# First four pooling tiles normalized inside the feed-forward's second pass; its results kept in SBUF and added by GpSimd; sums stored from SP

## The chip, the cores and the metric

One Trainium2 chip (trn2), one core of it. The metric is the device time of one execution in microseconds (us), lower is better. The engines are TensorE (PE, matmuls; PEld is its weight load), VectorE (DVE), ScalarE (ACT), GpSimd (POOL) and SyncE (SP, which here only issues DMAs). A DMA issued by SP is shown on the queue "hardware_dynamic", one issued by POOL on "software_dynamic".

## The reference

A two-layer backbone over 1024 tokens of width 1024, all in float32. Layer 0 is attention plus spatial gating and a dense SwiGLU feed-forward. Layer 1 begins with a pooling mixer and ends with a mixture of experts. The change sits between the two layers:

```python
x = x + mx[5] * _swiglu(_modulate(x, mx[3], mx[4]), w_gate, w_up, w_down)       # layer 0, dense feed-forward
...
x = x + mx[2] * _multiscale_pool(_modulate(x, mx[0], mx[1]), pool_w, pool_scale)  # layer 1, pooling mixer
x = x + mx[5] * _moe_swiglu(_modulate(x, mx[3], mx[4]), ...)                      # layer 1, experts
```

`_modulate(x, shift, scale)` is the row's RMS norm times (1 + scale) plus shift. `_multiscale_pool` takes, for four groups of 256 columns, centred means over 2, 4, 8 and 16 neighbouring tokens minus the token itself, multiplies each group by a 256x256 matrix and scales the columns.

## The kernel before, in words

The kernel is a sequence of phases. Each phase is a block with one instruction stream per engine; it ends with a barrier of all engines and a clearing of its semaphores by GpSimd (`phase_semaphores`), so that no engine begins a phase before every engine has finished the one before. Tokens are worked in tiles of 128 rows (`x[:, t, :]`, eight tiles).

**Feed-forward (`expert_mlp_phase` with the name "ffn").** Two passes of 512 tokens (four tiles); each pass runs 11 chunks of 256 hidden columns. In a chunk PE makes the gate and up products (`hidden`) and then the down products of the chunk before (`down`). ACT rounds weights and hidden values (`round_g`, `round_u`, `round_hidden`, `round_d`), DVE subtracts the rounded from the raw ones (`rest_g` and so on, L2413) and adds up the results in `y_t` (`add`, L2469). The chunks run in loops of pairs (`chunk_pairs`). At the end of a pass PE turns the sums, ACT and DVE write them to `y_out` (the tiles `dense_rows`, L2374 and L2584), and GpSimd adds each 128x1024 tile to the residual stream in DRAM (`x2`, shown as scratch_x) by an accumulating DMA (`add_result`, L2009). The DMAs of the last pass count up `dense_stored`. Rows of the tokens come in through `x_first`.

**Pooling (`pool_phase`).** SP loads the eight tiles of `x2` (L1232; the last four behind a wait on `dense_stored`), with shift and scale of layer 1 between the first and the second, and gate and column scales after them. For each tile: ACT squares and sums the row and takes the root (`first_norm`, L1310, L1312); DVE inverts it and modulates (`modulate`, L1379, L1388, L1389) into one of two buffers `h`; ACT rounds it to `h_hi` (`round_h`, L1316); DVE takes the rest `h_lo` (`split_h`, L1393). ACT also rounds the tables of the means (`band_hi` L1345, `edge_hi` L1346), and DVE their rest (`band_lo`, L1399). PE then multiplies by the tables (`difference`, L1267), turns the result (`turn`) and multiplies by the group matrices (`project`, L1291); a tile's `difference` needs `h` of the next tile too, so the first waits for two tiles. The order on ACT and DVE is written by hand: five tiles (`LEAD`) go ahead of PE, then one more in each step.

```python
            for t in range(LEAD):
                modulate(t)
                if t:
                    split_h(t - 1)
```

At the end of each tile DVE adds the gated result to x, ACT normalizes it for the experts (`norm`, L1343, `xn_rows`), and GpSimd stores both x and the normalized rows (L1244, L1245). GpSimd then waits until all sixteen stores have landed, and only then is the phase over.

**Routing (`routing_phase`)** begins with transposes of `xn_rows` on PE (L1536), and with SP's loads of the router's matrix (L1507) and of small tables.

## Time and profile before

| | |
|---|---|
| three runs, device time | 3943.25 to 3946.82 us, median 3946.48 |
| the profiled execution: its own time | 3940.43 us |
| its span, first to last instruction | 3938.4 us, mean granted TensorE clock 0.959 |
| busy share of the span | PE 92%, PEld 84%, DVE 58%, ACT 42%, POOL 8% |
| last matmul of the feed-forward to first of pooling | 1361.7 to 1396.2 us |
| pooling, first to last instruction | 1376.4 to 1470.0 us |
| first instruction of routing | 1475.6 us |

The profile is of one execution. Its times are microseconds from the start of the span. A row of the timeline gives start, duration, engine, line, operation and tiles, and in brackets how long the engine sat idle just before and on whom it waited. Windows give the busy time of each engine in a stretch, then the clock that was granted to TensorE (1.00 is the full 2.4 GHz, 0.50 is 1.2 GHz). Landing is the time from the issue of a DMA until its data are there.

### The profile page before, as it was taken

To read this page: it belongs to the slowest core of one execution; us is meant where nothing else is said; L and a number is where in the kernel's file an instruction comes from. 1 tells how busy PE (TensorE), PEld (TensorE's weight loads), DVE (VectorE), ACT (ScalarE), POOL (GpSimd) and SP (SyncE) were. 2 spreads that over 40 slices of the span, in tenths; PEclk is the share of its full clock that TensorE was granted. 3 is DMA by queue.
4 is the path that set the end of the run, shared out by engine and by line. 5 is a ranking of instruction groups with operands and counts; after the bars stand their busy time and mean duration, and the time that the engine had idled before them with its cause. 6 is when DMAs were issued, how large, how long until landed. Compare 5 with 4: busy or idle time off the path is not lost. (4 is left out here: it accounts for less than half of the span.)

```text
span 3938.4 us, 61110 instructions
## 1 busy us (share of the span) xinstructions
PE 3622.0 (92%) x22550; PEld 3318.8 (84%) x22551; DVE 2275.8 (58%) x2997; ACT 1662.4 (42%) x1943; POOL 296.5 (8%) x247
## 2 busy tenths in 40 slices
PE   7989897999999865999999999989999899999995
PEld 4986576888888653989999999988899898998995
DVE  3557634444444364866655555558565697665665
ACT  4225524222322153754443343347443465444444
POOL 0006401000000001010010010000100100000001
PEclk8999998999999987999999999999999999999997
DMA  6513325332322134974454354459543665545553
GB/s 220 214 56 113 121 75 202 98 98 96 107 96 96 46 147 147 357 236 173 160 174 140 137 162 138 143 165 367 184 156 131 182 245 183 181 160 150 199 174 137
DMA packets 408821, 627.11 MB, mean 159 GB/s; under 512 B 18227, under 2 KB 332211, under 8 KB 408616
## 3 DMA queue, kind: packets, MB, share of 16 engines
q1 hardware_dynamic: 384136, 534.68, 39.1%
q0 software_dynamic: 24192, 88.98, 7.7%
q8 instruction: 88, 1.44, 0.2%
q14 instruction: 117, 0.96, 0.1%
q10 hardware_dynamic: 288, 1.05, 0.1%
HBM read 579.46 MB, written 46.15 MB: 159 GB/s over the span
## 5 line engine op out<-in xcount | busy, mean ns | idle before, releaser
L2413 DVE TENSOR_TENSOR moe_gu_lo<-moe_raw_gu_lo,moe_gu_hi 128x2048 fp32r<-128x2048 f32 x254 | 580.7, 2286 | 160.9 <-ACT moe_gu_hi L2262 160.5
L2262 ACT ACTIVATE moe_gu_hi<-moe_raw_gu_lo 128x2048 fp32r<-128x2048 f32 x254 | 485.9, 1914 | 276.6 <-DMA moe_raw_gu_lo<-in_moe_w_gate 224.2
L2102 PE MATMUL moe_g<-moe_x,moe_gu_hi 128*128 128x336 f32 (+4 forms) x1344 | 416.9, 310 | 29.0 <-issue 20.3
L2469 DVE SCALAR_TENSOR_TENSOR moe_y_t<-moe_y,moe_cols,moe_y_t 128x288 f32<-128x288 f32 (+4 forms) x728 | 372.6, 536 | 105.7 <-PE moe_y L2104 105.1
L2104 PE MATMUL moe_g<-moe_x,moe_gu_lo 128*128 128x336 f32 (+4 forms) x1344 | 415.3, 309 | 0.0
L2103 PE MATMUL moe_g<-moe_x,moe_gu_hi 128*128 128x336 f32 (+4 forms) x1344 | 415.2, 309 | 0.0
L2102 PE MATMUL moe_y<-moe_h,moe_d_hi 128*128 128x336 f32 (+4 forms) x1344 | 412.5, 307 | 2.8 <-DVE moe_y_t L2465 2.8
L2102 PE MATMUL moe_u<-moe_x,moe_gu_hi 128*128 128x336 f32 (+4 forms) x1344 | 410.2, 305 | 0.0
L2104 PE MATMUL moe_u<-moe_x,moe_gu_lo 128*128 128x336 f32 (+4 forms) x1344 | 410.0, 305 | 0.0
L2104 PE MATMUL moe_y<-moe_h,moe_d_lo 128*128 128x336 f32 (+4 forms) x1344 | 409.9, 305 | 0.0
L2103 PE MATMUL moe_u<-moe_x,moe_gu_hi 128*128 128x336 f32 (+4 forms) x1344 | 409.6, 305 | 0.0
L2103 PE MATMUL moe_y<-moe_h,moe_d_hi 128*128 128x336 f32 (+4 forms) x1344 | 409.5, 305 | 0.0
L2449 DVE TENSOR_TENSOR moe_h_full<-moe_h_full,moe_u 128x336 f32<-128x336 f32 (+4 forms) x168 | 80.4, 479 | 483.8 <-PE moe_u L2104 483.8
L2413 DVE TENSOR_TENSOR moe_d_lo<-moe_raw_d_lo,moe_d_hi 128x2048 fp32r<-128x2048 f32 x126 | 287.7, 2284 | 10.8 <-ACT moe_d_hi L2262 10.8
L2102 PEld LDWEIGHTS moe_g<-moe_x,moe_gu_hi 128*128 128x128 f32 x1344 | 259.1, 193 | 31.1 <-issue 31.1
L2294 ACT ACTIVATE moe_h<-moe_h_full 128x336 fp32r<-128x336 f32 (+5 forms) x196 | 87.0, 444 | 456.9 <-DVE moe_h_full L2449 456.9
L2103 PEld LDWEIGHTS moe_g<-moe_x,moe_gu_hi 128*128 128x128 f32 x1344 | 258.4, 192 | 0.0
L2104 PEld LDWEIGHTS moe_g<-moe_x,moe_gu_lo 128*128 128x128 f32 x1344 | 258.4, 192 | 0.0
L2102 PEld LDWEIGHTS moe_y<-moe_h,moe_d_hi 128*128 128x128 f32 x1344 | 253.7, 189 | 3.5 <-DVE moe_y_t L2465 3.5
L2102 PEld LDWEIGHTS moe_u<-moe_x,moe_gu_hi 128*128 128x128 f32 x1344 | 254.0, 189 | 0.0
L2104 PEld LDWEIGHTS moe_u<-moe_x,moe_gu_lo 128*128 128x128 f32 x1344 | 253.3, 188 | 0.0
L2103 PEld LDWEIGHTS moe_u<-moe_x,moe_gu_hi 128*128 128x128 f32 x1344 | 253.2, 188 | 0.0
(388 smaller groups left out, 8169.3 us busy)
## 6 DMA issues: line engine op xcount, KB each, us to landing
moe_raw_gu_lo<-in_moe_w_gate SPq DMA_DIRECT2D x127, 1024.0 KB, 4.9
moe_raw_gu_lo<-in_moe_w_up SPq DMA_DIRECT2D x127, 1024.0 KB, 7.1
...
```

The costliest lines, as they stand in the source:

```text
L2102: pe.matmul(bank[:, 0:width], wh, moving[:, 0, 0:width], start=start, stop=False)
L2103: pe.matmul(bank[:, 0:width], wh, moving[:, 1, 0:width], start=False, stop=False)
L2104: return pe.matmul(bank[:, 0:width], wl, moving[:, 0, 0:width], start=False, stop=stop)
L2262: act.activation(hi[par][:, :, :], raw[par][:, :, :], ACT.Copy).then_inc(rounded, 1)
L2294: act.activation(h[par][:, f, 0, 0:width], h_full[:, f, 0:width], ACT.Copy).then_inc(h_rounded, 1)
L2413: dve.tensor_tensor(lo[par][:, :, :], raw[par][:, :, :], hi[par][:, :, :].bitcast(F), ALU.subtract).then_inc(split, 1)
L2449: dve.tensor_tensor(h_full[:, f, 0:width], h_full[:, f, 0:width], up, ALU.mult)\
L2469: dve.scalar_tensor_tensor(y_t[:, db, 0:cols], y_ps[db % 4][:, 0:cols], gate, y_t[:, db, 0:cols], ALU.mult, ALU.add).then_inc(y_added, 1)
```

## The change

1. **In the feed-forward's second pass** (`load_pooled`, `pooled_squares`, `pooled_roots`, `modulate_pooled`) the four tiles of tokens that the first pass has finished are normalized and modulated for pooling. GpSimd reloads them from `x2` into `x_first`, and shift and scale of layer 1 into two tiles of `y_out` that stand empty; ACT squares them between chunks 3 and 4 and between chunks 5 and 6 and takes all roots in one instruction; DVE modulates two tiles after chunk 7 and two after chunk 9. `chunk_pairs` of that pass is split on ACT (three loops for one) and on DVE (two for one).
2. **The last pass's results are not added in DRAM.** The four accumulating DMAs are gone; the tiles stay in `dense_rows`, and in pooling GpSimd adds them to the four loaded tiles (`added`). `x` of pooling (`keep["pool_x"]`) is no longer a tile of the phase alone.
3. **In pooling** ACT and DVE begin with the rounding and the rests of four tiles that are ready (`READY` = 4); only tile 4 is normalized ahead of the loop. SP loads tiles 4 to 7 first. The two squares' buffers are tiles of their own.
4. **SP stores** x and the normalized rows instead of GpSimd, and pooling no longer waits until they have landed: SP waits for them (`pool_stored`) in routing, behind its loads.

```diff
         @block.sync
         def _(sp):
-            for t in range(TX):
-                if t == TX - TILES_PASS:
-                    for stored in keep["dense_stored"]:
-                        sp.wait_ge(stored, 16)
+            for t in (*range(READY, TX), *range(READY)):
                 sp.dma_start(x[:, t, :], dram["x2"][t * P:(t + 1) * P, :]).then_inc(x_ld[t], 16)
-                if t == 0:
+                if t == READY:
                     for i, to in enumerate((shift, scale)):
                         sp.dma_start(to[:, :], dram["pool_mod"][i, :].partition_broadcast(P)).then_inc(mod_ld, 16)
...
+            for t in range(TX):
+                sp.wait_ge(normed, t + 1)
+                sp.dma_start(dram["x3"][t * P:(t + 1) * P, :], x[:, t, :]).then_inc(x_st, 16)
+                sp.dma_start(dram["xn"][t * P:(t + 1) * P, :], x_norm[:, t, :]).then_inc(x_st, 16)
 
         @block.gpsimd
         def _(pool):
 
-            for t in range(TX):
-                pool.wait_ge(normed, t + 1)
-                pool.dma_start(dram["x3"][t * P:(t + 1) * P, :], x[:, t, :]).then_inc(x_st, 16)
-                pool.dma_start(dram["xn"][t * P:(t + 1) * P, :], x_norm[:, t, :]).then_inc(x_st, 16)
-            pool.wait_ge(x_st, 32 * TX)
+            for t in range(READY, TX):
+                pool.wait_ge(x_ld[t], 16)
+                pool.tensor_tensor(x[:, t, :], x[:, t, :], keep["dense_rows"][:, t - READY, :], ALU.add).then_inc(added, 1)
...
+            round_h(0)
             act.activation(band_hi[:, :, :, :], band[:, :, :, :], ACT.Copy).then_inc(tables_ok, 1)
+            round_h(1)
             act.activation(edge_hi[:, :, :, :], edge[:, :, :, :], ACT.Copy).then_inc(tables_ok, 1)
+            for t in range(2, READY):
+                round_h(t)
             act.wait_ge(eps_ok, 1)
-            for t in range(LEAD):
-                first_norm(t)
-                if t:
-                    round_h(t - 1)
+            first_norm(READY)
             copy(0)
...
+            split_h(0)
+            dve.wait_ge(tables_ok, 1)
+            dve.tensor_tensor(band_lo[:, :, 0:3:2, :], band[:, :, 0:3:2, :], band_hi[:, :, 0:3:2, :].bitcast(F), ALU.subtract)\
+               .then_inc(band_ok, 1)
+            for t in range(1, READY):
+                split_h(t)
             dve.wait_ge(mod_ld, 32)
             link(dve.tensor_scalar(scale[:, :], scale[:, :], 1.0, None, ALU.add))
...
+            modulate(READY)
...
             sp.dma_start(tile_starts[:, :], dram["tile_starts"].partition_broadcast(P)).then_inc(ld, 16)
+            sp.wait_ge(keep["pool_stored"], 32 * TX)
...
+            def load_pooled():
+
+                pool.memset(pooled["early_eps"][:, :], EPS).then_inc(pool_ready, 1)
+                for t in range(TILES_PASS):
+                    pool.wait_ge(y_stored[t], 16)
+                    if t >= 2:
+                        pool.dma_start(y_out[:, t, :], pool_mod[t - 2, :].partition_broadcast(P)).then_inc(pool_mod_ld, 16)
+                pool.wait_ge(x_turned, passes * KD + X0)
+                for t in range(TILES_PASS):
+                    pool.dma_start(pool_h_in[:, t, :], x2[t * P:(t + 1) * P, :]).then_inc(pool_x_ld, 16)
...
+                def pooled_squares(tiles):
+
+                    act.wait_ge(pool_x_ld, TILES_PASS * 16)
+                    act.wait_ge(y_stored[1], 16)
+                    for t in tiles:
+                        if t:
+                            act.wait_ge(pool_squared, t)
+                        act.activation(pool_square, pool_h_in[:, t, :], ACT.Square, accum_out=pooled["early_sums"][:, t:t + 1])\
+                           .then_inc(pool_squared, 1)
...
+                if has_next(p):
+                    chunk_pairs(act, p, 0, C - 2, step)
+                else:
+                    chunk_pairs(act, p, 0, C - 8, step)
+                    pooled_squares(range(2))
+                    chunk_pairs(act, p, C - 7, C - 6, step)
+                    pooled_squares(range(2, TILES_PASS))
+                    pooled_roots()
+                    chunk_pairs(act, p, C - 5, C - 2, step)
...
+                def modulate_pooled(t):
+
+                    row = pool_h_in[:, t, :]
+                    dve.scalar_tensor_tensor(row, row, pooled["early_rstd"][:, t:t + 1], pool_scale, ALU.mult, ALU.mult)\
+                       .then_inc(pool_scaled, 1)
+                    dve.wait_ge(pool_scaled, t + 1)
+                    dve.tensor_tensor(row, row, pool_shift, ALU.add).then_inc(pool_h, 1)
...
+                    chunk_pairs(dve, p, 2, C - 4, step)
+                    dve.wait_ge(pool_mod_ld, 32)
+                    dve.tensor_scalar(pool_scale, pool_scale, 1.0, None, ALU.add).then_inc(pool_ready, 1)
+                    dve.wait_ge(pool_rooted, 1)
+                    dve.reciprocal(pooled["early_rstd"][:, :], pooled["early_root"][:, :]).then_inc(pool_ready, 1)
+                    dve.wait_ge(pool_ready, 3)
+                    modulate_pooled(0)
+                    modulate_pooled(1)
+                    chunk_pairs(dve, p, C - 3, C - 2, step)
+                    modulate_pooled(2)
+                    modulate_pooled(3)
```

How DVE's instructions stand at the start of pooling, before:

```order
L1395 MEMSET pool_eps 128x1
L1397 TENSOR_SCALAR pool_scale<-pool_scale 128x1024
L1399 TENSOR_TENSOR pool_band_lo<-pool_band,pool_band_hi 128x4x2x128
L1379 RECIPROCAL pool_rstd<-pool_root 128x1
L1388 SCALAR_TENSOR_TENSOR pool_scaled<-pool_x,pool_rstd,pool_scale 128x1024
L1389 TENSOR_TENSOR x_first<-pool_scaled,pool_shift 128x1024
L1379 RECIPROCAL pool_rstd<-pool_root 128x1
L1388 SCALAR_TENSOR_TENSOR pool_scaled<-pool_x,pool_rstd,pool_scale 128x1024
L1389 TENSOR_TENSOR x_first<-pool_scaled,pool_shift 128x1024
L1393 TENSOR_TENSOR pool_h_lo<-x_first,pool_h_hi 128x1024
```

and in the changed kernel, up to the first wait for a product of PE:

```order
L1401 MEMSET pool_eps 128x1
L1399 TENSOR_TENSOR pool_h_lo<-x_first,pool_h_hi 128x1024
L1404 TENSOR_TENSOR pool_band_lo<-pool_band,pool_band_hi 128x4x2x128
L1399 TENSOR_TENSOR pool_h_lo<-x_first,pool_h_hi 128x1024 x3
L1409 TENSOR_SCALAR pool_scale<-pool_scale 128x1024
L1386 RECIPROCAL pool_rstd<-pool_root 128x1
L1394 SCALAR_TENSOR_TENSOR pool_scaled<-pool_x,pool_rstd,pool_scale 128x1024
L1395 TENSOR_TENSOR x_first<-pool_scaled,pool_shift 128x1024
L1386 RECIPROCAL pool_rstd<-pool_root 128x1
L1394 SCALAR_TENSOR_TENSOR pool_scaled<-pool_x,pool_rstd,pool_scale 128x1024
L1395 TENSOR_TENSOR x_first<-pool_scaled,pool_shift 128x1024
L1399 TENSOR_TENSOR pool_h_lo<-x_first,pool_h_hi 128x1024
```

Behind the memset, twelve instructions and a wait for shift and scale stood ahead of the second `pool_h_lo`, which PE needs; now the first two `pool_h_lo` and `pool_band_lo` are DVE's first three operations.

How GpSimd's instructions stand around the end of the feed-forward and in pooling, before (the pair L1244, L1245 comes eight times in all):

```order
L2009 DMA scratch_x<-dense_rows 128x1024 x8
L1786 UNCONDITIONAL_BRANCH
L101 ISA
L1239 UNCONDITIONAL_BRANCH
L1244 DMA scratch_x<-pool_x 128x1024
L1245 DMA scratch_xn<-xn_rows 128x1024
```

and in the changed kernel:

```order
L2022 DMA scratch_x<-dense_rows 128x1024 x4
L2026 MEMSET early_eps 128x1
L2030 DMA dense_rows<-scratch_pool_mod 128x1024 x2
L2033 DMA x_first<-scratch_x 128x1024 x4
L1795 UNCONDITIONAL_BRANCH
L101 ISA
L1243 UNCONDITIONAL_BRANCH
L1248 TENSOR_TENSOR pool_x<-pool_x,dense_rows 128x1024 x4
```

GpSimd leaves the feed-forward with loads that belong to the start of the second pass as its last DMAs, and in pooling it computes where it stored.

## Rows read from the trace of the kernel before

**Rows 1.** Windows: busy us (count) per engine, TensorE clock, DMA share, GB/s
```profile
1100.00:1300.00 200.00, 200.00 (x884) 165.62 (x883) 89.44 (x90) 48.54 (x43) 0.00 (x0) 1.00 0.29 94
...
1361.00:1367.00 6.00, 0.66 (x7) 0.42 (x4) 1.21 (x2) 0.60 (x1) 2.55 (x3) 1.00 0.99 158
1367.00:1396.00 29.00, 0.00 (x0) 0.00 (x0) 11.80 (x14) 12.29 (x18) 0.00 (x0) 0.50 0.79 257
1396.00:1401.00 5.00, 4.63 (x20) 4.34 (x20) 4.84 (x7) 3.11 (x7) 0.00 (x0) 0.50 0.00 0
1401.00:1466.00 65.00, 55.58 (x356) 50.46 (x356) 45.60 (x55) 40.74 (x73) 6.36 (x12) 1.00 0.25 98
```

**Rows 2.** Timeline at the feed-forward's end, and landing of its four accumulating DMAs
```profile
1361.70 0.69 DVE L2584 TENSOR_SCALAR dense_rows<-ffn_y 128x512 f32<-128x512 f32 x1 [0.18 <-PE ffn_y L2162]
...
DMA to landing us min/median/max: 5.4/9.3/12.3
```

**Rows 3.** Timeline at the boundary from attention to its output phase
```profile
469.69 0.42 DVE L786 COPY att<-att_out_ps 128x256 f32<-128x256 f32 x1 [1.42 <-PE att_out_ps L740]
470.84 0.37 SPq L935 DMA_DIRECT2D mix_w_s<-in_gm_w_s  x1
```

**Rows 4.** Timeline of ACT, DVE and PE at the start of pooling
```profile
1376.45 1.48 ACT L1345 ACTIVATE pool_band_hi<-pool_band 128x1536 fp32r<-128x1536 f32 x1 [14.60 <-PEq L102]
...
1379.87 1.06 ACT L1310 ACTIVATE x_first<-pool_x 128x1024 f32<-128x1024 f32 x1 [0.99 <-DMA pool_x<-scratch_x]
...
1381.04 1.28 ACT L1312 ACT_TABLE_LOAD   x1
...
1385.27 1.06 ACT L1310 ACTIVATE x_first<-pool_x 128x1024 f32<-128x1024 f32 x1 [2.65 <-DMA pool_x<-scratch_x]
...
1391.16 1.22 DVE L1393 TENSOR_TENSOR pool_h_lo<-x_first,pool_h_hi 128x1024 fp32r<-128x1024 f32 x1
...
1396.25 0.58 PE L1267 MATMUL pool_diff_ps<-pool_h_hi,pool_band_hi 128*128 128x256 f32 x1 [34.59 <-DVE pool_h_lo L1393]
```

**Rows 5.** Timeline of POOL and DVE in the output phase
```profile
3907.39 10.25 POOL L1733 TENSOR_TENSOR moe_y<-moe_y,moe_rows 128x1024 f32<-128x1024 f32 x4 [257.34 <-POOLq L102]
...
3912.01 3.43 DVE L1763 SCALAR_TENSOR_TENSOR out_early<-out_early,out_rstd,out_gain 128x1024 f32<-128x1024 f32 x1
...
3915.54 3.18 DVE L1763 SCALAR_TENSOR_TENSOR out_early<-out_early,out_rstd,out_gain 128x1024 f32<-128x1024 f32 x1
...
3918.83 1.28 DVE L1763 SCALAR_TENSOR_TENSOR out_early<-out_early,out_rstd,out_gain 128x1024 f32<-128x1024 f32 x1
```

**Rows 6.** Timeline of PE in pooling: a stall that has nothing ahead of it
```profile
1421.76 0.36 PE L1267 MATMUL pool_diff_ps<-pool_h_hi,pool_band_hi 128*128 128x256 f32 x1 [1.58 <-ACT pool_diff L1328]
```

**Rows 7.** Timeline from pooling to routing, and landing of the stores of xn_rows
```profile
1467.52 1.15 ACT L1343 ACTIVATE xn_rows<-pool_x,pool_rstd 128x1024 f32<-128x1024 f32 x1 [0.30 <-DVE pool_rstd L1379]
...
1469.49 0.53 POOL L1245 DMA_DIRECT2D scratch_xn<-xn_rows  x1
...
1475.59 0.38 SPq L1507 DMA_DIRECT2D route_router<-in_router_w  x1
...
1478.07 1.78 PE L1526 MATMUL route_logit_t_ps<-route_h,route_router 128*8 128x512 f32 x2 [0.49 <-DMA route_router<-in_router_w]
...
DMA to landing us min/median/max: 3.8/3.8/3.8
```

**Rows 8.** Timeline of ACT, DVE and PE late in the second pass
```profile
1286.66 0.60 ACT L2287 ACTIVATE ffn_h_full<-ffn_g 128x512 f32<-128x512 f32 x1 [8.67 <-PE ffn_g L2104]
...
1292.10 0.69 DVE L2449 TENSOR_TENSOR ffn_h_full<-ffn_h_full,ffn_u 128x512 f32<-128x512 f32 x1 [7.75 <-PE ffn_u L2104]
1292.70 2.29 DVE L2413 TENSOR_TENSOR ffn_gu_lo<-ffn_raw_gu_lo,ffn_gu_hi 128x2048 fp32r<-128x2048 f32 x1
...
1313.66 0.39 PE L2102 MATMUL ffn_g<-ffn_x,ffn_gu_hi 128*128 128x512 f32 x1
```

**Rows 9.** Waits of the whole span: ACT's time in which it waited for nothing shown
```profile
ACT L2262 <- issue: 86.6, 9, 15.1
```

87 lines of the change are left out of this document (52 added, 35 removed).

## The prediction

> **What bounds the kernel now.** I read the windows first, because the busy share of the whole span says nothing about a stage. In the feed-forward PE is busy 200.00 of 200.00 us, with DVE at 89.44 and ACT at 48.54 [rows 1]: there PE is the bound and the other two have room. From 1367 to 1396 PE is at zero; from 1401 to 1466, in pooling, it is busy 55.58 of 65 us, DVE 45.60 and ACT 40.74 [rows 1]. So the places to win are the hole before pooling and the joints, and inside pooling PE paces again.
>
> The timeline names what ends the hole: PE sits 34.59 us until DVE's `pool_h_lo` [rows 4], and it splits it. DVE's last work in the feed-forward ends at 1361.70 + 0.69 = 1362.39, and nothing of pooling starts before ACT at 1376.45, after 14.60 us of idling [rows 4]; the accumulating DMAs, issued around 1360 to 1364, take up to 12.3 us to land [rows 2], and DMAs are busy 0.99 of the time there [rows 1]. That is 14.1 us of joint. At the joint from attention to its output phase, where GpSimd has no DMA in flight, last work and first work are 470.11 and 470.84, 0.73 us apart [rows 3]. I read the 13.3 us between the two as GpSimd not leaving its phase before its own DMAs are done. Then 1376.45 to 1396.25, 19.8 us, pass inside pooling until PE starts: loads, and norms and modulations on ACT and DVE [rows 4]. At the end ACT is done at 1467.52 + 1.15 = 1468.67 and routing begins at 1475.59: 6.9 us, of which most is the last store, issued at 1469.49 and 3.8 us in landing [rows 7].
>
> **The change, part by part.** The sum is made against the profiled execution, 3940.4 us; the median of the runs, 3946.5, stands 6.1 us above it, and I carry the difference over to the median.
>
> *Work moved into the second pass: 0.* ACT gets four squares (1.06 us each in pooling [rows 4], with the reading of the sum a little more), two at a place, with the root behind the second pair, some 4 us, and table changes in the loop after it; DVE gets two modulations at a place, 4 x about 1.25 plus a scale and an inversion, some 6 us. ACT idles 8.67 us and DVE 7.75 us while PE makes a chunk's first products, and weights split by 1292.70 + 2.29 = 1294.99 are first used at 1313.66, 18.7 us later [rows 8]. Nothing else waits for these rows until pooling. The cover is that slack; without it the whole work would show: on ACT 4 x 1.25 for squares, 0.3 for the root and five table loads of 1.28 [rows 4], 11.7 us; on DVE 4 x 2.5 + 0.9 = 10.9 us. GpSimd's six loads (3 MB) come right after the first pass's additions, when the next thing anybody needs of them is four chunks off; on GpSimd nothing is queued behind them.
>
> *Joint to pooling: -13.3.* No DMA of GpSimd is in flight at the end now, so 14.1 us should become 0.73. Bounds: -13.3, and -11.8 if the joint costs what the one after pooling costs beyond the landing (1469.49 + 3.8 = 1473.3 to 1475.59, 2.3 us [rows 7]).
>
> *Start of pooling until PE's first product: -12.5.* What must come first now is two roundings and two tables on ACT, and three subtractions on DVE. ACT: h(0) at 1.0 us, `band_hi` to 2.4, h(1) to 3.4, `edge_hi` to 4.4 (1.48 us for the wide table and 1.06 for a tile [rows 4], each overlapping the next by some 0.1). DVE: h_lo(0) to 2.2, `band_lo` 2.4 to 3.6, h_lo(1) to 4.8. So PE could start at 4.8 instead of 19.8: -15.0. But the first of tiles 4 to 7 arrives where tile 0 does now, 3.4 us into the phase (1379.87 against 1376.45 [rows 4]), and then GpSimd adds, 10.25 / 4 = 2.56 us each [rows 5]. In the output phase DVE's 128x1024 operation with two tiles from SBUF lasts 1.28 us alone but 3.43 and 3.18 us while GpSimd adds [rows 5]. The first addition starts just when h_lo(1) is due, and holds it to about 6.1; PE starts at 7.3. Bounds: 4.8 without the meeting, 7.3 with it; I take 7.3, since the output phase shows the same pair of operations.
>
> The Trainium skill ("SBUF — State Buffer", SBUF: two separate sides) says that the port pair which VectorE and GpSimd share is an exclusive lock, held for the whole instruction, also against a VectorE operation with two SBUF inputs: the loser fully blocks. It speaks against this change; the trace agrees (3.43 for 1.28 us). Taken to its end, it gives the rival of full cost below.
>
> *Rest of pooling: +1.0.* PE's order is untouched, its products are the same, and its stall of 1.58 us behind ACT's copy [rows 6] comes from tile 6's modulation standing behind the first result on DVE, which stays so. The granted clock was 0.50 when PE restarted at 1396.25, with PE idle since about 1361.7, and 1.00 from 1401 [rows 1]; before, it was still 1.00 up to 1367. PE will be idle some 9 us now, past that point, so I assume the same slow 5 us. New is that additions 2 to 4, from about 8.8 us on (second tile now: 1385.27 - 1376.45 [rows 4]), meet tile 4's modulation, and ACT must round it before it copies tile 1's differences. That copy is due at about 16 us. A modulation that takes two blocks of 2.0 us ends between 14 and 17. Bounds -1.6 (the stall gone) and +2.6 (one whole addition more); I take +1.0.
>
> *Joint to routing: -5.2.* SP issues the last two stores in 0.4 us each (0.38 for its router load [rows 7]) and goes; 0.9 + 0.73 = 1.7 us after ACT instead of 6.9. *Router's matrix: +1.5.* PE already waits 0.49 us for it, 2.5 us after its issue [rows 7]. Now 1 MB of stores is ahead of it, landing 3.8 us after the last issue, 4.7 us after ACT's end, where the router used to need 1.7 + 2.4 = 4.1. So it comes between 0 and 3.0 us later than it could (0.6 to 3.0 if it queues); I take 1.5. Small tables are needed much later. The Trainium skill ("DMA: Bandwidth & Descriptors", Queues, rings and completion order) says that an engine consumes a ring's descriptors in order, and by it the sum would have the upper half of that range; no row here shows it.
>
> Sum: -13.3 - 12.5 + 1.0 - 5.2 + 1.5 = **-28.5 us**. That is 3911.9 for an execution like the profiled one, and 3946.5 - 28.5 = **3918.0** for the median.
>
> **The rivals.** *Forecast, 58%: 3918.0.*
>
> *The additions miss DVE, 13%.* If tile 4 lands late or DVE wins the race for the start, PE begins at 4.8 and nothing is delayed later: -13.3 - 15.0 - 5.2 + 1.5 = -32.0, 3914.5. For it: a delay of half a microsecond in the load decides. Against: the blocks in the output phase were not avoided by DVE once [rows 5].
>
> *Each addition costs the path in full, 16%.* Four additions by 2.0 us (3.43 and 3.18 less 1.28 [rows 5]) make 8.1 in place of the 3.5 that I count: -23.9, 3922.6. DVE would be the bound of the first 20 us. Against: between the additions DVE waits for roots anyway. This is what the lock rule of the Trainium skill's SBUF page makes of it if all four meet DVE.
>
> *The joint does not shrink, 6%.* If the 14.1 us are not the accumulating DMAs but code loading or another fixed cost of leaving this phase, then -28.5 + 13.3 = -15.2, 3931.3. Against: the other joint with 0.73 us [rows 3].
>
> *The change does not hide what it moves, 4%.* If the 12 us on ACT and 11 us on DVE stand on PE's path, -28.5 + 23 = -5.5, 3941.0, which is no change. Against: 200.00 us busy of 200.00 with DVE at 45% [rows 1].
>
> *Slower, 3%.* ACT enters two loops more in the second pass and DVE one, three new pieces of code. ACT's wait for nothing shown reaches 15.1 us elsewhere [rows 9]. Each such stall is free up to 18.7 us [rows 8] and stops PE beyond. The change is lost when each of the three takes 18.7 + 28.5/3 = 28.2 us, and slower by 0.2% from 31 us; at 35 us each it would be 3946.5 - 28.5 + 3 x 16.3 = 3966.9. It would need twice the longest stall on record.
>
> **How the numbers follow.** About 0.2% of this kernel, 7.9 us, is what a measurement can tell from no change. The range: all good ends are -13.3 - 15.0 - 1.6 - 5.2 + 0 = -35.1 (3911.4), all bad ends of the forecast are -11.8 - 12.5 + 2.6 - 5.2 + 3.0 = -23.9 (3922.6), which is also the time of the rival of full cost. The runs of the kernel before spread over 3.6 us, and a TensorE clock that stays low some 5 us longer would cost about 2.5; I set 3908 to 3928, which leaves out the joint, the unhidden work and the slower case, 13%, and a little. Faster by over 0.2%: 58 + 13 + 16 + 6 = 93%; within: 4%; slower: 3%.
>
> **What would show it.** Right: pooling's first instruction 0.7 to 2.3 us after the feed-forward's last; PE's first difference about 7 us later with DVE's second `pool_h_lo` at 3 us or more; `TENSOR_TENSOR pool_x` on POOL about 2.6 us; the same PE pace after that; routing 1.7 us after ACT, PE waiting for the router 1 to 3 us; PE in the second pass 100% busy at clock 1.00. Wrong: a joint of over 5 us, a gap of PE in the second pass, PE's first difference before 5.5 or after 9 us, or a pooling phase whose steps from one gated result to the next are longer than before.

## The result, and the profile after

| | before | changed |
|---|---|---|
| median device time | 3946.32 us (4 runs, 3943.25 to 3946.82) | 3906.67 us (4 runs, 3902.22 to 3907.56) |
| profiled execution, its span | 3940.43 us, 3938.4 | 3906.23 us, 3904.5 |
| ratio of the times | | 0.9896, 95% interval 0.9881 to 0.9910 |

The change is faster by 39.65 us where 28.5 were forecast. The time lies 1.3 us below the range. So the direction was right and the size was not, and as the stages show the sum was wrong in both directions: one term gave back more than I had allowed for, and a stage that the change does not touch got shorter. How much shorter the kernel is differs between series of runs as well: in a later one the same two kernels took 3940.14 and 3908.84 us, 31.3 us apart (ratio 0.9919, 0.9904 to 0.9933; the run a_again below).

**Where the time went, by stage.** I cut both profiled executions at the same eight events. Each cut can be read in the rows; those of after follow below.

| stretch, us | before | after | difference | forecast |
|---|---|---|---|---|
| start to DVE's last result of the feed-forward | 1362.39 | 1363.24 | +0.85 | 0 |
| from there to pooling's first instruction on ACT | 14.06 | 0.91 | -13.15 | -13.3 |
| to PE's first product | 19.80 | 7.04 | -12.76 | -12.5 |
| to the end of ACT's last `xn_rows` | 72.42 | 78.42 | +6.00 | +1.0 |
| to SP's load of the router's matrix | 6.92 | 1.77 | -5.15 | -5.2 |
| routing, up to GpSimd's first copy for the experts | 56.64 | 58.39 | +1.75 | +1.5 |
| experts' phase, up to GpSimd's additions of the output | 2375.16 | 2364.11 | -11.05 | 0 |
| output, to the end of the span | 31.01 | 30.62 | -0.39 | 0 |
| sum | 3938.4 | 3904.5 | -33.9 | -28.5 |

The medians lie further apart than these two executions, since the profiled one of before was 5.9 us under its median and the one of after only 0.4. The +0.85 of the first line is scatter: in the other executions of kernels whose feed-forward is that of before, the same point lies between 1361.8 and 1365.1 us.

The windows of the changed kernel, with the columns of [rows 1], show that the moved work is hidden: in 200 us that hold the first three groups of moved work, PE is still busy all the time at clock 1.00, while ACT rose from 48.54 to 61.44 and DVE from 89.44 to 95.06.

```profile
1090.00:1290.00 200.00, 200.00 (x884) 165.62 (x883) 95.06 (x96) 61.44 (x58) 0.00 (x0) 1.00 0.29 96
```

The timeline at the joint answers to [rows 2, 4]: DVE's last result of the feed-forward, ACT's first rounding, and PE's first product.

```profile
1362.55 0.69 DVE L2658 TENSOR_SCALAR dense_rows<-ffn_y 128x512 f32<-128x512 f32 x1 [0.18 <-PE ffn_y L2188]
...
1364.15 1.06 ACT L1321 ACTIVATE pool_h_hi<-x_first 128x1024 fp32r<-128x1024 f32 x1 [1.44 <-PEq L102]
...
1371.19 0.58 PE L1270 MATMUL pool_diff_ps<-pool_h_hi,pool_band_hi 128*128 128x256 f32 x1 [8.68 <-DVE pool_h_lo L1399]
```

The next rows are the place where 5 us more than forecast went: the timeline of DVE, GpSimd, ACT and PE in the first 21 us of pooling.

```profile
1367.45 2.61 POOL L1248 TENSOR_TENSOR pool_x<-pool_x,dense_rows 128x1024 f32<-128x1024 f32 x1 [352.17 <-DMA pool_x<-scratch_x]
1372.79 8.96 POOL L1248 TENSOR_TENSOR pool_x<-pool_x,dense_rows 128x1024 f32<-128x1024 f32 x3 [2.74 <-DMA pool_x<-scratch_x]
...
1367.76 5.66 DVE L1399 TENSOR_TENSOR pool_h_lo<-x_first,pool_h_hi 128x1024 fp32r<-128x1024 f32 x3
1373.33 2.87 DVE L1409 TENSOR_SCALAR pool_scale<-pool_scale 128x1024 f32<-128x1024 f32 x1
...
1376.43 3.13 DVE L1394 SCALAR_TENSOR_TENSOR pool_scaled<-pool_x,pool_rstd,pool_scale 128x1024 f32<-128x1024 f32 x1
1379.60 3.25 DVE L1395 TENSOR_TENSOR x_first<-pool_scaled,pool_shift 128x1024 f32<-128x1024 f32 x1
...
1382.95 1.28 DVE L1394 SCALAR_TENSOR_TENSOR pool_scaled<-pool_x,pool_rstd,pool_scale 128x1024 f32<-128x1024 f32 x1
...
1382.88 1.06 ACT L1321 ACTIVATE pool_h_hi<-x_first 128x1024 fp32r<-128x1024 f32 x1 [5.56 <-DVE x_first L1395]
1383.84 1.06 ACT L1333 ACTIVATE pool_diff<-pool_diff_ps 128x512 f32<-128x512 f32 x2
...
1385.05 0.55 PE L1270 MATMUL pool_diff_ps<-pool_h_hi,pool_band_hi 128*128 128x256 f32 x1 [4.97 <-ACT pool_diff L1333]
```

The last three additions come back to back, 8.96 us, and three DVE operations in a row, the scale and tile 4's modulation, take 2.87, 3.13 and 3.25 us; the same operation as the second takes 1.28 as soon as GpSimd has stopped, in the row at 1382.95. Tile 4 is late by that. ACT has to round tile 4 before it copies tile 1's differences, so it idles 5.56 us and then copies, and PE, which had caught up, waits 4.97 us for that copy. The windows after it show a second price: TensorE's granted clock falls back to 0.50 in the stretch where PE restarts, as it had at the first start. In the timeline PE's first 15 products from 1385.05 on take 3.28 us, where later ones start every 0.12 us; that is about 1.5 us lost (an estimate from these rows).

```profile
1382.00:1384.00 2.00, 0.00 (x0) 0.00 (x0) 1.96 (x3) 1.12 (x2) 0.00 (x0) 1.00 0.06 23
1384.00:1386.00 2.00, 0.95 (x4) 0.98 (x5) 1.97 (x3) 2.00 (x5) 0.00 (x0) 0.70 0.00 0
1386.00:1388.00 2.00, 2.00 (x12) 2.00 (x11) 0.63 (x1) 1.97 (x4) 0.00 (x0) 0.50 0.00 0
1388.00:1390.00 2.00, 2.00 (x18) 2.00 (x18) 0.00 (x0) 1.07 (x3) 0.00 (x0) 0.94 0.00 0
```

The joint to routing, beside [rows 7]: routing begins 1.77 us after ACT, and PE waits 0.94 us for the router's matrix, which was 0.49.

```profile
1448.46 1.15 ACT L1348 ACTIVATE xn_rows<-pool_x,pool_rstd 128x1024 f32<-128x1024 f32 x1 [0.30 <-DVE pool_rstd L1386]
...
1451.38 0.38 SPq L1515 DMA_DIRECT2D route_router<-in_router_w  x1
...
1454.31 1.88 PE L1535 MATMUL route_logit_t_ps<-route_h,route_router 128*8 128x512 f32 x2 [0.94 <-DMA route_router<-in_router_w]
```

The matrix thus costs 0.45 of routing's 1.75 us. The rest goes with TensorE's clock. Windows of before, from 4.4 us into routing, and of the changed kernel, from 3.6 to 10.6 us into it:

```profile
1480.00:1500.00 20.00, 20.00 (x79) 6.66 (x78) 0.68 (x1) 10.10 (x13) 0.00 (x0) 1.00 0.04 8
```

```profile
1455.00:1462.00 7.00, 7.00 (x20) 2.15 (x18) 0.00 (x0) 1.91 (x3) 0.00 (x0) 0.65 0.12 22
```

In windows of 2 us the changed kernel still has 0.50 from 1456 to 1458 and 0.52 from 1458 to 1460, up to 8.6 us into the phase. DVE's first copy of the router's products comes 17.39 us into routing and came 15.10 us into it before; about half a microsecond of that is made up by the end of the phase.

**The experts' phase** is bounded by two rows of GpSimd, of before (the second is the first of [rows 5]):

```profile
1532.23 0.19 POOL L2705 COPY token_now<-token_of 128x4 int32<-128x4 int32 x1 [62.21 <-POOLq L1994]
```

and of the changed kernel:

```profile
1509.77 0.19 POOL L2783 COPY token_now<-token_of 128x4 int32<-128x4 int32 x1 [128.01 <-POOLq L2008]
...
3873.88 11.24 POOL L1742 TENSOR_TENSOR moe_y<-moe_y,moe_rows 128x1024 f32<-128x1024 f32 x4 [253.85 <-POOLq L102]
```

Nothing in the code of this phase differs. What differs is in the waits. Of before, ACT's idle time without a releaser at L2262 is 86.6 us with a longest of 15.1 [rows 9], and PE has this row:

```profile
PE moe_u L2192 <- DVE moe_h_full L2483: 14.3, 4, 8.5
```

In the changed kernel the two read:

```profile
ACT L2288 <- issue: 52.3, 9, 8.9
...
PE moe_u L2218 <- DVE moe_h_full L2536: 10.9, 5, 3.4
```

The timeline has one such pair. Before, at the end of a pass of the experts, ACT finishes at 2621.48 and begins the next chunk at 2631.60, 10.12 us in which it waited for nothing that the profile knows; PE stands still for 8.53 us up to 2638.88, until DVE has worked on what ACT prepares after that.

```profile
2620.79 0.69 ACT L2374 ACTIVATE moe_y<-moe_y,weight_now 128x512 f32<-128x512 f32 x1 [0.66 <-PE moe_y L2162]
...
2631.60 1.28 ACT L2262 ACT_TABLE_LOAD   x1 [10.12 <-issue]
...
2638.88 0.69 PE L2192 MATMUL moe_u<-ident,moe_h_full 128*128 128x128 f32 x2 [8.53 <-DVE moe_h_full L2483]
```

After, at the same place of the same pass, ACT waited 4.80 us:

```profile
2597.59 0.69 ACT L2427 ACTIVATE moe_y<-moe_y,weight_now 128x512 f32<-128x512 f32 x1 [0.67 <-PE moe_y L2188]
...
2603.08 1.28 ACT L2288 ACT_TABLE_LOAD   x1 [4.80 <-issue]
```

The queue q14, which the profile names "instruction", carried less, 117 packets before and 101 after.

That gave Theory 1: the change put 71 more instructions on ACT and 49 more on DVE ahead of the experts' code (a count of the two programs), and where this code lies in memory sets how long an engine waits for it. The rival was that the phase differs by chance from execution to execution.

### The profile page after: what moved, and what is told of

It is laid out like the page before. It is cut to its first block and busy times, and to the rows that moved or that the text cites. A ratio compares the mean times of both kernels' runs of the same rounds, so it can differ in the third digit from the quotient of the medians.

```text
span 3904.5 us, 61076 instructions
## 1 busy us (share of the span) xinstructions
PE 3620.8 (93%) x22550; PEld 3316.3 (85%) x22551; DVE 2284.8 (59%) x2995; ACT 1668.4 (43%) x1945; POOL 300.9 (8%) x238
## 5 line engine op out<-in xcount | busy, mean ns | idle before, releaser
L2128 PEld LDWEIGHTS moe_y<-moe_h,moe_d_hi 128*128 128x128 f32 x1344 | 253.1, 188 | 2.0 <-DVE moe_y_t L2518 2.0
L2130 PEld LDWEIGHTS moe_y<-moe_h,moe_d_lo 128*128 128x128 f32 x1344 | 253.7, 189 | 0.0
L2129 PEld LDWEIGHTS moe_y<-moe_h,moe_d_hi 128*128 128x128 f32 x1344 | 253.2, 188 | 0.0
```

The costliest lines, as they stand in the source:

```text
L2128: pe.matmul(bank[:, 0:width], wh, moving[:, 0, 0:width], start=start, stop=False)
L2129: pe.matmul(bank[:, 0:width], wh, moving[:, 1, 0:width], start=False, stop=False)
L2130: return pe.matmul(bank[:, 0:width], wl, moving[:, 0, 0:width], start=False, stop=stop)
```

## The experiments

The expectations speak of "the experts' phase" with its ends taken between the first and last instruction of a phase, which gives 0.1 us more than the table above. Most runs were executed several times and have an interval against the kernel before on the same chip; the three runs on the joint and a_double are one execution each.

### Padding: code moved, nothing else

An unused semaphore is increased on ACT at the end of routing and on DVE at its start; "b_" is made from the kernel before, "a_" from the changed one. The change also moved GpSimd's and SP's code, by 12 instructions fewer and 14 more; the padding leaves that out.

```diff
+            for _ in range(71):
+                act.sem_inc(padded[0], 1)
...
+            for _ in range(49):
+                dve.sem_inc(padded[1], 1)
```

> The kernel before with nothing of the change, but with 71 semaphore increments added on ScalarE behind its last work in routing and 49 on VectorE ahead of its first work there, both while the engine waits, so that the experts' code stands as many instructions further on as in the changed kernel. Theory 1 (the expert phase's 11 us come from where its code stands): from routing's end to the output phase 2364 us instead of 2375, ScalarE's idle time with nothing shown to wait for some 52 us instead of 87, and the whole 7 to 12 us faster than before. Theory 2 (the 11 us are a difference between executions, or come from the rows' stores going through SP): 2375 us there, time within 3 us of before.

> The changed kernel with 185 increments more on ScalarE and 207 more on VectorE at the same two places of routing. Theory 1: the expert phase changes again, by some us in either direction (toward 2375 us if the place repeats itself every 256 instructions, since 71 + 185 and 49 + 207 are 256), so 3900 to 3920 us. Theory 2: 2364 us in the expert phase and 3906 to 3908 us in all.

> The kernel before with 71 increments of an unused semaphore on ScalarE alone, at the end of routing. With the increments on both ScalarE (71) and VectorE (49) the phase of the experts took 2367.4 us instead of 2375.2. Theory: ScalarE's code place sets it, since ScalarE's idle time at L2262 without a releaser fell most (86.6 to 48.0 us in its group): then this run gives the whole gain, experts' phase 2366 to 2369 us and 3930 to 3934 us in all. Rival: VectorE's place sets it: then this run is like the kernel before, 2374 to 2376 us and 3940 to 3944. Second rival: each has a share.

> The kernel before with 49 increments on VectorE alone, at the start of routing. Theory (ScalarE's place): nothing, experts' phase 2374 to 2376 us, 3940 to 3944 us in all. Rival (VectorE's place): the whole gain, 2366 to 2369 us, 3930 to 3934.

| run | ACT, DVE moved by | median | before, same chip | ratio (95%) | experts' phase | ACT's idle time without releaser at the experts' weights: sum, longest | q14 packets |
|---|---|---|---|---|---|---|---|
| before | 0, 0 | 3946.32 | | | 2375.2 | 86.6, 15.1 | 117 |
| b_pad | 71, 49 | 3932.51 | 3942.54 | 0.9975 (0.9965 to 0.9985) | 2367.3 | 48.0, 8.8 | 101 |
| b_pad_act | 71, 0 | 3934.88 | 3941.91 | 0.9980 (0.9971 to 0.9989) | 2364.8 | 53.7, 8.7 | 107 |
| b_pad_dve | 0, 49 | 3938.79 | 3941.91 | 0.9993 (0.9984 to 1.0002) | 2373.6 | 74.4, 13.5 | 110 |
| changed | 71, 49 | 3906.67 | 3946.32 | 0.9896 (0.9881 to 0.9910) | 2364.1 | 52.3, 8.9 | 101 |
| a_pad | 256, 256 | 3917.80 | 3942.54 | 0.9936 (0.9922 to 0.9949) | 2377.7 | 76.7, 14.9 | 121 |

The cuts of b_pad, from the timeline of GpSimd, and its row of the waits:

```profile
1535.23 0.19 POOL L2710 COPY token_now<-token_of 128x4 int32<-128x4 int32 x1 [61.78 <-POOLq L1999]
...
3902.52 11.24 POOL L1738 TENSOR_TENSOR moe_y<-moe_y,moe_rows 128x1024 f32<-128x1024 f32 x4 [259.59 <-POOLq L102]
...
ACT L2267 <- issue: 48.0, 8, 8.8
```

Increments that do nothing make the kernel before faster by 10.0 us, with an interval clear of 1. In the changed kernel others go the other way: a_pad's ratio, 0.9936, is clear of the changed kernel's 0.9896, but it is not clear of that kernel's 0.9919 in a later series (0.9904 to 0.9933), so its size is open; the medians are 9 to 11 us apart. So the place of the code moves the time. ACT's part is the larger one by the medians, 7.0 us; DVE's 3.1 us has an interval that includes no effect, so whether it has a share is not decided; the two together agree with b_pad. Moved by 256, ACT's longest wait is back where it was at 0 (14.9 for 15.1 us), which fits places that repeat every 256 instructions, but one point does not prove a period.

How much of the 11.05 us is it? The length of the phase in one execution does not say. The profiled execution of b_pad_act was the fastest of its eleven, 7.8 us under their median, and that of b_sp_stores, a run below that moves nothing on ACT and DVE, has 2370.5 us with ACT's waits as long as before (88.2, longest 14.8). A window over the phase splits it into the time in which PE is busy with its 15648 products and the time in which it is not:

| experts' phase, us | length | PE busy | PE idle |
|---|---|---|---|
| before, place 0 | 2375.2 | 2253.3 | 121.9 |
| b_sp_stores, place 0 | 2370.5 | 2244.0 | 126.5 |
| b_pad, place 71 | 2367.3 | 2253.0 | 114.3 |
| b_pad_act, ACT alone at 71 | 2364.8 | 2244.3 | 120.5 |
| b_pad_dve, DVE alone at 49 | 2373.6 | 2250.4 | 123.2 |
| changed, place 71 | 2364.1 | 2249.5 | 114.6 |
| a_again, place 71 | 2368.8 | 2253.4 | 115.4 |
| a_both_p57, place 128 | 2376.7 | 2252.7 | 124.0 |
| a_pad, place 256 | 2377.7 | 2252.4 | 125.3 |

PE's busy time differs by up to 9 us between executions, whatever the place; it is scatter. The idle time goes with the place: 121.9 and 126.5 us at 0, 114.3 to 119.5 in the nine executions with both engines at their places in the changed kernel or within four instructions of them, 124.0 at 128 and 125.3 at 256. So of the 11.05 us between the two profiled executions, 7.3 are less idle time, as in b_pad (7.6), and 3.7 are scatter of the executions. That ACT alone has the larger part rests on the medians; in b_pad_act's one profile PE's idle time is only 1.4 us below that of before.

### What holds a phase open: GpSimd's own DMAs

Three kernels look at the joint behind the feed-forward. Made from the changed one, they copy or add the last four tiles to unused rows in DRAM as well, and nobody but GpSimd, behind its additions, waits for them.

```diff
+                for t in range(TILES_PASS):
+                    pool.wait_ge(y_left, (passes - 1) * TILES_PASS + t + 1 + O0)
+                    pool.wait_ge(y_right, (passes - 1) * TILES_PASS + t + 1 + O0)
+                    pool.dma_start(pooled["x3_spare"][t], y_out[:, t, :]).then_inc(pooled["copy_stored"], 16)
...
+            pool.wait_ge(keep["copy_stored"], 16 * TILES_PASS)
```

In a_joint_sp the same three lines stand on SP; in a_joint_acc the DMA has `accum_op=ALU.add`, onto rows filled in the first chunks of the second pass.

> The changed kernel with four 128x1024 tiles of the feed-forward's last pass also copied to unused rows in DRAM by GpSimd's own DMAs, as late as before, and waited for only in pooling by GpSimd behind its additions. Nobody waits for these data at the joint. Theory: GpSimd itself doesn't leave a phase while its own DMAs are in flight; then the joint from the feed-forward's last instruction to pooling's first is 12 to 14 us again instead of 0.9, and the whole 3917 to 3921 us. Rival: the joint was long because someone waited for the data of the accumulating DMAs; then it stays 0.9 us, and the whole is within 2 us of 3906.

> The same four copies, issued by SP on the hardware queue at the same place. Theory: only GpSimd's own DMAs hold it; the joint stays 0.9 us, at most 1 to 2 us more for the four issues, the whole 3905 to 3909 us. Rival: any DMA in flight at the end of a phase holds it, 12 to 14 us, the whole 3917 to 3921 us.

> The changed kernel with the four tiles of the last pass added to unused rows in DRAM by GpSimd with an accumulating DMA, as before the change but with nobody waiting for them except GpSimd behind its additions. The plain copies on the same queue landed in 3.6 us and the joint was 6.1 us from VectorE's end; from SP's queue 1.4 us. Theory: GpSimd leaves the phase when its own DMAs have landed, and accumulating ones take 9 us; then VectorE's end to pooling's first instruction is 12 to 15 us. Rival: the accumulation itself doesn't matter, 6 us as with the copies, and the rest of the 14 us before was the wait of SP for the data.

DVE's last row of the feed-forward, ACT's first of pooling, and the copies with their median time to landing, of a_joint_pool:

```profile
1362.26 0.69 DVE L2663 TENSOR_SCALAR dense_rows<-ffn_y 128x512 f32<-128x512 f32 x1 [0.18 <-PE ffn_y L2193]
...
1369.04 1.06 ACT L1322 ACTIVATE pool_h_hi<-x_first 128x1024 fp32r<-128x1024 f32 x1 [6.62 <-PEq L102]
...
scratch_x<-dense_rows POOLq DMA_DIRECT2D x4, 512.0 KB, 3.6
```

of a_joint_sp, with PE's first product and GpSimd's first addition:

```profile
1361.36 0.69 DVE L2664 TENSOR_SCALAR dense_rows<-ffn_y 128x512 f32<-128x512 f32 x1 [0.18 <-PE ffn_y L2194]
...
1363.48 1.06 ACT L1322 ACTIVATE pool_h_hi<-x_first 128x1024 fp32r<-128x1024 f32 x1 [1.96 <-PEq L102]
...
1368.35 0.58 PE L1271 MATMUL pool_diff_ps<-pool_h_hi,pool_band_hi 128*128 128x256 f32 x1 [7.04 <-DVE pool_h_lo L1400]
...
1368.81 3.43 POOL L1248 TENSOR_TENSOR pool_x<-pool_x,dense_rows 128x1024 f32<-128x1024 f32 x1 [354.53 <-DMA pool_x<-scratch_x]
...
scratch_x<-dense_rows SPq DMA_DIRECT2D x4, 512.0 KB, 3.1
```

and of a_joint_acc:

```profile
1363.86 0.69 DVE L2666 TENSOR_SCALAR dense_rows<-ffn_y 128x512 f32<-128x512 f32 x1 [0.18 <-PE ffn_y L2196]
...
1377.83 1.06 ACT L1322 ACTIVATE pool_h_hi<-x_first 128x1024 fp32r<-128x1024 f32 x1 [13.80 <-PEq L102]
...
scratch_x<-dense_rows POOLq DMA_DIRECT2D x4, 512.0 KB, 8.8
```

| | DVE's end to ACT's start | the profiled execution |
|---|---|---|
| changed | 0.91 | 3906.2 |
| copies from SP | 1.43 | 3902.0 |
| copies from GpSimd | 6.09 | 3913.3 |
| additions in DRAM from GpSimd | 13.28 | 3924.1 |
| before | 14.06 | 3940.4 |

My expectation for the copies from GpSimd, 12 to 14 us, missed: I had taken the landing time of the accumulating DMAs (median 9.3 us [rows 2]) for that of any DMA. The two others came in at the joint. These are single executions, but the joint scatters little: 0.91 us in the changed kernel and in five others whose GpSimd has nothing in flight there, 12.0 to 14.1 in the five kernels that keep the additions of before. The joint follows the landing of GpSimd's own DMAs, 3.6 us each or 8.8, though nobody waits for the data. The same copies from SP hold almost nothing: the last was issued at 1362.1, none landed in under 2.7 us, and pooling began at 1363.48, while it was under way. The 14 us were thus two facts at once: GpSimd doesn't leave the phase while its DMAs are under way, and adding in DRAM takes more than twice as long as copying. Which of GpSimd's instructions does the waiting no row shows.

a_joint_sp also answers another question. There the first addition began at 1368.81, after the second `pool_h_lo` (1.22 us, ended at 1368.30), and PE's first product came 4.87 us into pooling instead of 7.04, with the additions still on GpSimd. So it is the meeting of these two that costs PE's start 2.2 us.

### The stall in pooling: two repairs

a_dve_add gives the four additions to DVE, at the places where it would otherwise wait; a_act_order leaves them on GpSimd and lets ACT round tile 4 only after it has copied tile 1's differences.

```diff
-            for t in range(READY, TX):
-                pool.wait_ge(x_ld[t], 16)
-                pool.tensor_tensor(x[:, t, :], x[:, t, :], keep["dense_rows"][:, t - READY, :], ALU.add).then_inc(added, 1)
...
+            def add_rows(t):
+                dve.wait_ge(x_ld[t], 16)
+                dve.tensor_tensor(x[:, t, :], x[:, t, :], keep["dense_rows"][:, t - READY, :], ALU.add).then_inc(added, 1)
```

```diff
-                if t + LEAD <= TX:
+                if t and t + LEAD <= TX:
                     round_h(t + LEAD - 1)
...
                 copy_turned(t)
+                if t == 0:
+                    round_h(LEAD - 1)
```

> The changed kernel with the four additions of the kept rows on VectorE instead of GpSimd: tile 4's behind the second rest, tile 5's ahead of tile 4's modulation, the other two behind tile 4's rest. If VectorE is held by GpSimd's additions: all its 128x1024 operations at the start of pooling take 1.1 to 1.3 us, TensorE's first difference comes 4.8 us into the phase instead of 7.0, its stall of 5.0 us behind ScalarE's copy goes, and pooling is 6 to 8 us shorter; 3899 to 3901 us. If the additions are hidden whatever engine does them: no change or up to 3 us more, for 4 x 1.15 us more on VectorE.

> The changed kernel with one instruction moved on ScalarE: tile 4's rounding behind the copies of the first step instead of ahead of them. If TensorE's 5.0 us stall comes from the copy standing behind a rounding that waits for VectorE: the stall goes, the granted clock does not fall again at 1385, and pooling is 4 to 6 us shorter with VectorE's operations still stretched to 3.1 us; 3901 to 3903 us. If VectorE is the bound of the start anyway: under 1 us.

> The changed kernel with the additions on VectorE and with tile 4's rounding behind the copies of the first step on ScalarE, the two edits measured singly. The additions on VectorE gave 2.2 us before PE's first product and 4.4 us behind it, the order on ScalarE 6.4 us behind it. Theory: both shorten the same stall of PE near 20 us into pooling (GpSimd's and VectorE's crossing makes tile 4 late, ScalarE's order passes that on to PE), so behind PE's first product no more than 7 us go, and with the 2.2 us before it some 9 us in all in pooling; 3896 to 3902 us if the experts' phase stays 2364 to 2368 us. Rival: two separate stalls, the gains add, 13 us, 3892 to 3895.

| us | pooling's first instruction to PE | PE to ACT's last `xn_rows` | both | experts' phase | median | ratio (95%) |
|---|---|---|---|---|---|---|
| before | 19.80 | 72.42 | 92.2 | 2375.2 | 3946.32 | |
| changed | 7.04 | 78.42 | 85.5 | 2364.1 | 3906.67 | 0.9896 (0.9881 to 0.9910) |
| a_dve_add | 4.9 | 74.0 | 78.9 | 2368.0 | 3902.76 | 0.9895 (0.9880 to 0.9910) |
| a_act_order | 7.0 | 72.0 | 79.0 | 2366.7 | 3903.75 | 0.9898 (0.9882 to 0.9913) |
| a_both | 4.9 | 74.2 | 79.1 | 2370.2 | 3902.36 | 0.9900 (0.9885 to 0.9915) |

The timeline of a_dve_add, PE's first product, the second addition between the scale and tile 4's modulation on DVE, and ACT's end:

```profile
1369.60 0.58 PE L1268 MATMUL pool_diff_ps<-pool_h_hi,pool_band_hi 128*128 128x256 f32 x1 [6.52 <-DVE pool_h_lo L1397]
...
1372.87 0.69 DVE L1413 TENSOR_SCALAR pool_scale<-pool_scale 128x1024 f32<-128x1024 f32 x1
1373.69 1.23 DVE L1401 TENSOR_TENSOR pool_x<-pool_x,dense_rows 128x1024 f32<-128x1024 f32 x1
...
1375.03 1.29 DVE L1392 SCALAR_TENSOR_TENSOR pool_scaled<-pool_x,pool_rstd,pool_scale 128x1024 f32<-128x1024 f32 x1
...
1442.48 1.15 ACT L1346 ACTIVATE xn_rows<-pool_x,pool_rstd 128x1024 f32<-128x1024 f32 x1 [0.30 <-DVE pool_rstd L1384]
```

Without GpSimd beside it, the scale is back at 0.69 us for 2.87 and the modulation at 1.29 for 3.13, and an addition costs DVE 1.23 us, less than the 2 us that one on GpSimd costs it in waiting. In a_act_order the DVE operations are as long as in the changed kernel:

```profile
1375.66 3.08 DVE L1396 SCALAR_TENSOR_TENSOR pool_scaled<-pool_x,pool_rstd,pool_scale 128x1024 f32<-128x1024 f32 x1
1378.77 3.31 DVE L1397 TENSOR_TENSOR x_first<-pool_scaled,pool_shift 128x1024 f32<-128x1024 f32 x1
```

but the chain from them to PE is cut, the granted clock stays at 1.00 from 1376 on, and pooling is as short. Each repair takes 6.4 to 6.6 us off the whole of pooling, and both together no more (79.1): they remove one stall, not two. That is even less than the 9 us that I expected of both, since the 2.2 us before PE's first product are lost again behind it. The windows show where. In the changed kernel the clock is back at 1.00 in the window that begins 4.8 us after PE's first product; in a_dve_add it is still 0.50 in the one that begins 6.4 us after it, and 0.86 in the next:

```profile
1376.00:1378.00 2.00, 1.90 (x16) 1.93 (x17) 1.93 (x3) 1.29 (x3) 2.00 (x1) 1.00 1.03 412
```

```profile
1376.00:1378.00 2.00, 2.00 (x11) 2.00 (x11) 1.93 (x4) 0.79 (x4) 0.00 (x0) 0.50 1.03 414
```

PE starts earlier and then works some 5 us longer at half the clock, about 2 us lost by an estimate from these rows; a_both has the same 0.50 there. Why the clock comes back later in these two is not shown.

The whole, expected at 3899 to 3901, 3901 to 3903 and 3896 to 3902 us, came out at 3902.76, 3903.75 and 3902.36, each a little above. Their ratios are that of the changed kernel in its first series (0.9896) and better than the one in a later series (0.9919), so the 6.4 us are shown in the stage and not in the whole. The experts' phase was 3 to 6 us longer than 2364.1 in these executions, but the changed kernel itself had 2368.8 in another, so nothing follows from that.

### The stores moved alone

b_sp_stores is the kernel before with part 4 of the change only: SP stores, and waits for the landing in routing.

> The kernel before with only part 4 of the change: SP stores x and the normalized rows, pooling doesn't wait for their landing. Theory: the joint from pooling to routing shrinks by 5 us as in the changed kernel (from 5.6 to 1.0 us behind the last instruction), routing gives 1 to 2 us back while PE waits for the router's matrix behind the stores, 3 to 4 us faster in all apart from the experts' phase. Rival: SP's loads queue behind the stores and routing gives it all back, 0.

3937.47 us against 3940.48 on the same chip, ratio 0.9996 (0.9987 to 1.0005), which doesn't tell the 3 to 4 us expected from nothing. Its stages do, with the cuts of the first table: from ACT's last `xn_rows` to SP's load 1.74 us for 6.92, and routing 58.33 for 56.64, PE waiting 0.99 us for the router's matrix and the clock at 0.50 up to 7.6 us into the phase. That is -5.2 and +1.7, the same as in the changed kernel, so both terms belong to this part. It changes two things at once, though, the engine that stores and the wait for the landing, which the kernel before had in its code; which of them held the phase is not separated.

### Is the moved work hidden with room

a_double squares each of the four tiles twice and modulates it twice in the second pass.

> The changed kernel with each of the four tiles squared twice on ScalarE and modulated twice on VectorE inside the feed-forward's second pass: about 4 us more on ScalarE and 16 us more on VectorE. Theory: the second pass is bound by TensorE and both have more slack than that; the feed-forward stays 749.8 us, within 0.5. Rival (the work moved there is hidden only just): the feed-forward grows by 2 to 15 us.

The window of the feed-forward's two passes, of a_double:

```profile
600.00:1363.00 763.00, 738.36 (x3301) 611.62 (x3300) 368.32 (x376) 232.85 (x230) 16.36 (x24) 0.98 0.33 108
```

and of the changed kernel:

```profile
600.00:1363.00 763.00, 738.29 (x3301) 611.49 (x3300) 358.36 (x368) 228.32 (x222) 16.31 (x24) 0.98 0.33 108
```

DVE did 9.96 us more (I had written 16; four modulations of 2.5 us are 10) and ACT 4.53, and the last result of the feed-forward came at 1363.31 instead of 1363.24. The cover has room for twice the work. (The whole took 3912.35 us, and the experts' phase of that execution 2370.2.)

### Looking for a better place

The version with both repairs was run with 57, 20 and 226 more increments on ACT, and the changed kernel once more on the chip of the last two.

> The same kernel with 57 increments of an unused semaphore on ScalarE at the end of routing. So far ScalarE's code moved by 71 instructions gave 8 to 11 us in the experts' phase and by 256 nothing; this run stands at 128. Theory (ScalarE's code place, returning every 256 instructions): another value of the experts' phase, between 2360 and 2378 us, which differs from that of the same kernel without increments by more than 2 us. Rival (a place is either good or bad by chance of the execution): within 2 us of it.

> The version with both edits and 20 increments on ScalarE, so that its code stands at 91 against the kernel before; 71 gave 2364 to 2370 us in the experts' phase, 128 gave 2377, 0 and 256 2375 to 2378. Theory (the cost of a place changes smoothly with it): 2364 to 2374 us and 3898 to 3908 in all. Rival (a place near 71 isn't special; single places are good): anything from 2360 to 2378.

> The same version with 226 increments, which is the place 297, or 41 if places return every 256 instructions. Theory: a value between those of 0 and 71, 2366 to 2374 us. Rival: no return every 256, any value from 2360 to 2378; at 256 it was 2377.7.

> The changed kernel itself, on the chip of the next two. Theory (the pooling stage of the version with both edits is 6.4 us shorter and its experts' phase 6 us longer): the two kernels are within 2 us of each other, 3902 to 3907 us where the kernel before takes 3940 to 3943. Rival: the edits are worth their 6 us in the whole, this kernel is 5 to 7 us above the better of the next two.

| run | ACT moved by | median | before, same chip | ratio (95%) | experts' phase | ACT, longest | q14 packets |
|---|---|---|---|---|---|---|---|
| a_both | 71 | 3902.36 | 3940.48 | 0.9900 (0.9885 to 0.9915) | 2370.2 | 9.2 | 100 |
| a_both_p57 | 128 | 3910.82 | 3940.48 | 0.9926 (0.9912 to 0.9939) | 2376.7 | 14.0 | 110 |
| a_both_p20 | 91 | 3904.50 | 3940.14 | 0.9905 (0.9889 to 0.9922) | 2370.3 | 8.2 | 86 |
| a_both_p226 | 297 | 3905.05 | 3940.14 | 0.9908 (0.9891 to 0.9925) | 2370.5 | 7.9 | 99 |
| a_again (changed) | 71 | 3908.84 | 3940.14 | 0.9919 (0.9904 to 0.9933) | 2368.8 | 9.2 | 100 |

Place 128 is worse by 8.5 us than 71 with the same work, so the place matters here too, and ACT's longest idle time, 14.0 us, and the packets are up with it. Places 91 and 297 are alike, neither better than 71; PE is idle for 121.2 and 120.8 us of the experts' phase there, and for 117.8 in a_both. With a_again a caution: the same kernel had 2364.1 us in one execution and 2368.8 in another, 3.9 of the 4.6 us in PE's busy time, so a difference of 4 us in the length of this phase between single executions is not a finding. And the packets alone don't give the time: 86 of them went with the same 2370 us as 100.

On one chip the repaired version at place 91 took 3904.50 and the changed kernel 3908.84 us, 4 us apart, where I had expected 2 at most and the rival 5 to 7; the intervals of the two ratios overlap, 0.9889 to 0.9922 and 0.9904 to 0.9933. The repaired version is the best so far by its medians, by 0.1%, and that is not told apart from equal.

## Why the prediction was right or wrong

*Work moved into the second pass, 0: right.* PE stayed busy 200.00 us of 200.00; the doubled work shows the room.

*Joint to pooling, -13.3: right,* -13.15, and for the reason given, which a_joint_pool, a_joint_sp and a_joint_acc show by themselves. The rival that the joint doesn't shrink is refuted.

*Start of pooling until PE's first product, -12.5: right,* -12.76. I had PE at 7.3 us and it started at 7.04; the first addition met the second `pool_h_lo` as described. Without that meeting PE started at 4.9 us, in a_dve_add and in a_joint_sp, for the 4.8 that stood in the prediction.

*Rest of pooling, +1.0 with bounds -1.6 to +2.6: failed,* it was +6.0. The step was "A modulation that takes two blocks of 2.0 us ends between 14 and 17", with ACT's copy of tile 1's differences due at 16. The modulation ended at 1382.85, 18.7 us in. Additions 2 to 4 began at 8.6 us, as forecast (8.8), but ran back to back, and there were three blocks, not two: the first fell on the scale, which has a single SBUF input and which I had counted as free. The three DVE operations lasted 2.18, 1.85 and 2.02 us longer than alone, 6.05 in sum, and ACT's order handed 4.97 us of it to PE. On top came a second stretch at clock 0.50, about 1.5 us, which I had not thought of because I had not thought of a second stop. The first one was shorter than the 5 us that I carried over: PE's 21st product came 4.91 us after its first, and 5.41 before. These three, 4.97 + 1.5 - 0.5, are the 6.0.

The rival of full cost named this mechanism and priced it at 8.1 us instead of 3.5, 3922.6 in all; by pooling alone (-6.76 from both steps, where forecast and that rival have -11.5 and -6.9) the rival was the one that happened, at 16%. That it fits within 0.2 us is in part luck: DVE lost 8.2 us by the four additions, as priced, but PE saw only 7.1 of them, and the clock, which that rival did not have, made up the rest. The Trainium skill ("SBUF — State Buffer", SBUF: two separate sides) counts also an operation in a two-port mode with one input as a party to the lock, not only one with two inputs; the scale's 2.87 us against 0.69 without GpSimd agrees. I had used half of that rule.

*Joint to routing, -5.2: right,* -5.15. *Router's matrix, +1.5: the number right by luck,* routing grew by 1.75. The matrix came only 0.45 us later, less than the 0.6 that I had as the least if it queues behind the stores; the other 1.3 go with TensorE's clock, which stayed at 0.50 up to 8.6 us into routing, and for which I had no term.

*The experts' phase, no term: this is the step that put the time below the range.* The sum takes everything behind the router's matrix as unchanged, and the range has no bound for it. Measured were -11.05 us between the two profiled executions, of which PE's idle time has -7.3 and the scatter of the executions the rest, and -10.0 in the medians (-13.8 to -5.9 by the interval) when the kernel before gets the same displacement of ACT's and DVE's code by padding. I did name code loading, as the slower rival, with L2262's rows [rows 9] as its evidence; the rows spoke of the experts' phase, and I asked only what new loops in the feed-forward would add, not what moving all later code would do to the waits that were already there. A term for moved code with bounds of about -10 to +3 belonged into the range, if the medians of b_pad (-10.0) and the phase of a_pad (2.5 us longer than before) are taken as its ends.

*The sum.* By the stages that I worked out it was -23.3 where I had -28.5, 5 us less than forecast. With padding's -10.0 that makes -33.3, which lies between the two differences that were measured, -39.65 and, in a later series, -31.3. The forecast of -28.5 lies near the second one because two errors of 5 and 10 us have opposite signs, which is luck. The larger difference of the first series comes in part from the kernel before: its median there was 3946.32, and 3940.14 to 3942.54 in the four later ones. I had also carried the 6.1 us between the profiled execution and the median over to the changed kernel, which assumes that it is the same in both; it was 5.9 and 0.4.
